# A two-block model on one core: order of ScalarE's table loads in the HGRN recurrence, three weight casts moved, nine filler matmuls and a bank turn

## What is computed

```python
# block 1
u = rms_norm(h, norm_mix_w)
q_a, k_a, v_a, f_a, q_h, f_h, i_h, g_h, gate_a, gate_h = split(u @ w_in)
y_a = forgetting_attention(...) @ w_attn_out                   # 8 heads of 64
f_val = lb + (1 - lb) * sigmoid(f_h); log_f = log(f_val); k = 1 - f_val
o_h = hgrn2_recurrence(q_h, log_f, k, i_h)                     # 8 heads of 128
o_h = rms_norm(o_h, hgrn_norm_w) * sigmoid(g_h)
mixed = sigmoid(gate_a) * y_a + sigmoid(gate_h) * (o_h @ w_hgrn_out)
h = h + mixed @ w_o
h = h + hierarchical_moe(rms_norm(h))                          # 32 experts, top 2
x = rms_norm(h)[:, 16:]
# block 2
h = h + 0.5 * rmsnorm(swiglu(rmsnorm(h, n0), ffn1_wi, ffn1_wo), n1)     # 2816 wide
h = h + rmsnorm(hybrid_mixer(rmsnorm(h, n2)), n3)   # Fourier, short conv, delta net
h = h + 0.5 * rmsnorm(swiglu(rmsnorm(h, n4), ffn2_wi, ffn2_wo), n5)
```

## Time and profile before

| | |
|---|---|
| Runs | 2757.00, 2758.17, 2758.91 us |
| Median | 2758.17 us |
| Profiled execution, its own time | 2753.36 us |
| Its span in the trace | 2752.0 us |
| Mean granted PE clock | 0.989 of full |
| PE busy | 2632.0 us, 96% |
| PEld busy | 2069.1 us, 75% |
| DVE busy | 1288.1 us, 47% |
| ACT busy | 888.8 us, 32% |
| ACT_TABLE_LOAD | 78 times 1283 ns |

### The profile page before, as it was taken

The page is one execution under the profiler, slowest core; times in us unless marked ns, Lnnn a source line. Parts: engine busy times, 40 slices in busy tenths (PEclk is TensorE's granted clock), DMA queues, the critical chain, the costliest instruction groups (busy, mean ns, idle before and its releaser), DMA issues.

```text
span 2752.0 us, 38590 instructions
## 1 busy us (share of the span) xinstructions
PE 2632.0 (96%) x16264; PEld 2069.1 (75%) x16264; DVE 1288.1 (47%) x2277; ACT 888.8 (32%) x1320; POOL 148.9 (5%) x201
## 2 busy tenths in 40 slices
PE   8999999999999989999999999999999999899997
PEld 6778787778744333359999999888979776688885
DVE  4446566534423333355343465454444433644444
ACT  4334445333221111133222242444435322431322
POOL 0000000000100000000000000132140400000000
PEclk9999999999999999999999999999999999999998
DMA  4012111134599999963222222211111122223221
GB/s 142 16 63 67 57 58 62 58 138 137 208 412 420 421 420 420 420 279 110 86 93 93 78 83 76 96 51 58 51 58 51 61 90 93 92 92 98 93 88 58
DMA packets 78203, 381.62 MB, mean 139 GB/s; under 512 B 9944, under 2 KB 10200, under 8 KB 52816
## 3 DMA queue, kind: packets, MB, share of 16 engines
q1 hardware_dynamic: 71856, 357.14, 35.3%
q0 software_dynamic: 5456, 20.11, 1.9%
q10 hardware_dynamic: 720, 1.90, 0.2%
HBM read 372.67 MB, written 10.62 MB: 139 GB/s over the span
## 4 chain that ended last, share of the span: by engine, by line
PE 74%; DMA 8%; DVE 4%; ACT 2%; SPq 2%; issue 1%; DVEq 0%; POOLq 0%; ACTq 0%
PE ps L208 72%; DMA rmore<-in_w_ein 5%; DMA ring<-in_w_ein 2%; SPq L293 2%; PE ps L212 1%; ACT L218 1%; DVE ringr L581 0%; DMA vrow<-uT 0%; PE ps L1958 0%; DMA ring<-in_w_hg 0%; DVE uT L472 0%; DVE hT L2660 0%; ACT ringr L575 0%; DMA xg<-vrow,idx 0%; ACT hdd L1227 0%
## 5 line engine op out<-in xcount | busy, mean ns | idle before, releaser
L208 PE MATMUL ps<-uh,ringr 128*128 128x264 f32 (+1 forms) x2256 | 552.7, 340 | 7.2 <-DVE mgb L3946 5.1
L208 PEld LDWEIGHTS ps<-uh,ringr 128*128 128x128 f32 x2256 | 366.2, 189 | 50.9 <-issue 8.6
L208 PE MATMUL ps<-buh,ringr 128*128 128x512 f32 (+1 forms) x1312 | 347.0, 351 | 10.0 <-ACT hg L1209 8.9
L208 PE MATMUL ps<-uTr,ringr 128*128 128x512 f32 (+1 forms) x1136 | 351.3, 346 | 0.0
L581 DVE TENSOR_TENSOR ringr<-ring,ringr 128x1024 fp32r<-128x1024 f32 (+1 forms) x215 | 258.2, 1212 | 141.8 <-ACT ringr L575 141.5
L208 PEld LDWEIGHTS ps<-buh,ringr 128*128 128x128 f32 x1312 | 218.7, 189 | 41.1 <-issue 13.0
L575 ACT CAST ringr<-ring 128x1024 fp32r<-128x1024 f32 (+1 forms) x215 | 219.3, 1036 | 87.2 <-DMA ring<-in_w_fi 33.5
L208 PEld LDWEIGHTS ps<-uTr,ringr 128*128 128x128 f32 x1136 | 197.7, 189 | 22.8 <-issue 3.1
L208 PE MATMUL ps<-ful,ringr 128*128 128x264 f32 (+1 forms) x648 | 169.6, 322 | 0.2 <-DVE ful L508 0.2
L2621 DVE TENSOR_TENSOR fsg<-ps,fsg 128x528 f32<-128x528 f32 (+1 forms) x44 | 30.8, 700 | 198.5 <-PE ps L208 195.1
L208 PE MATMUL ps<-fhh,ringr 128*128 128x264 f32 (+1 forms) x576 | 123.6, 321 | 0.0
(11 more groups left out here) (485 smaller groups left out, 4557.9 us busy)
## 6 DMA issues: line engine op xcount, KB each, us to landing
rmore<-in_w_ein SPq DMA_DIRECT2D x51, 1024.0 KB, 27.0
eahead<-in_w_ein SPq DMA_DIRECT2D x47, 1024.0 KB, 26.7
ring<-in_w_ein SPq DMA_DIRECT2D x30, 1024.0 KB, 27.0
rmore<-in_w_eout SPq DMA_DIRECT2D x27, 1024.0 KB, 27.0
ring<-in_w_fi SPq DMA_DIRECT2D x54, 512.0 KB, 3.7
ring<-in_w_eout SPq DMA_DIRECT2D x19, 1024.0 KB, 27.3
eahead<-in_w_eout SPq DMA_DIRECT2D x18, 1024.0 KB, 27.1
fmore<-in_w_fi SPq DMA_DIRECT2D x34, 512.0 KB, 3.8
```

The lines of the kernel that those rows point to most:

```text
L208: return self.P.matmul(out, lhsT, rhs, start=start, stop=stop, skip_group_check=True)
```

## The change

The tanh table is loaded right behind the logarithm in `project_act`. The root leaves `output_act` (beat 7) and becomes a method of its own, called at beat 6 between the two groups of steps. `Ffn.act` casts pieces 4, 5 and 6 before the norm's root. Nine filler matmuls stand before the first product of round 1 in `ConvFourier.pe`. In `MixerEnd.pe` the turn is set to 2 ahead of the eight products, so that the first takes banks 4 and 5.

```diff
@@ Hgrn.act
                 if h >= 2:
                     self.output_act(h - 2, n)
                 fill(STEPS[h][0])
+                if h >= 2 and n == 6:
+                    self.root_act(h - 2)
                 if h < 9 and n == 7:
                     self.turn_act(h - 1)
                 fill(STEPS[h][1])
@@ Hgrn.project_act
         A.activation(self.lf, self.fs, ACT.Ln).then_inc(self.f_log.next(), 1)
+        k.table(ACT.Tanh)
         for _ in range(5):
             yield 1
@@ Hgrn.output_act
-        if n == 7:
-            k.table(ACT.Ln)
-            A.wait_ge(*self.sum.at(h + 1))
-            if h:
-                A.wait_ge(*self.fin.at(h))
-            rb = k.rb[:, 0:S]
-            A.activation(rb, k.ps[:, self.bank["sum", h], :], ACT.Ln, bias=k.eps[:, 0:1], scale=1.0 / 128).then_inc(
-                self.o_log.next(), 1)
-            A.wait_ge(*self.o_log.last())
-            A.activation(rb, rb, ACT.Exp, scale=-0.5).then_inc(self.root.next(), 1)
+
+    def root_act(self, h):
+        k, A = self.k, self.k.A
+        k.table(ACT.Ln)
+        A.wait_ge(*self.sum.at(h + 1))
+        if h:
+            A.wait_ge(*self.fin.at(h))
+        rb = k.rb[:, 0:S]
+        A.activation(rb, k.ps[:, self.bank["sum", h], :], ACT.Ln, bias=k.eps[:, 0:1], scale=1.0 / 128).then_inc(
+            self.o_log.next(), 1)
+        A.wait_ge(*self.o_log.last())
+        A.activation(rb, rb, ACT.Exp, scale=-0.5).then_inc(self.root.next(), 1)
@@ Ffn.act
-        W.ahead_act(0, 5)
+        for i in range(4, 7):
+            W.cast_act(i)
         self.norm.root_act()
@@ ConvFourier.pe
         for j in range(4):
+            if j == 1:
+                k.busy(7, 9)
             for x in (3, 0, 1, 2) if j else (2,):
@@ MixerEnd.pe
         k.busy(banks[0], 9)
+        k.turn = 2
         for m in range(8):
```

## The result

The changed kernel took **2725.1 us** (median of four runs, 2724.83 to 2726.81) against 2757.6 us for the kernel before (four runs, 2755.94 to 2758.91): ratio 0.9884, 95% interval 0.9867 to 0.9901. The forecast was 2731.1 us, its range 2726 to 2741. The direction was right; the medians are 32.5 us apart where 27.1 were forecast.

What follows compares the result with a forecast made beforehand. PE, busy 96% of the span, was taken as the bound, gaining only where it waits or runs at lower clock. Terms summed to 27.1 us: 2753.36 to 2726.3 profiled, 2758.17 to 2731.1 us median; range 2726 to 2741.

Steps and rivals of the forecast that it cites:

- 1. to 3., recurrence: Odd passes: tanh load earlier 5.1 us, root earlier 3.1 us, full clock in pass 3 1.6 us; 9.8 us.
- late weight cast: Recurrence, odd passes: a late weight cast or DVE ends the wait for hg next, leaving 2.6 of 5.1 us.
- Terms 1 and 2: Recurrence: tanh load ahead in passes 1, 3, 5, 7 gains 5.1 us; root ahead in passes 3, 5, 7 gains 3.1.
- 4. New loads at nothing: Recurrence: eight loads behind hlf cost nothing, given 2.56 us idle in pass 4 and 3.4 us cover in pass 3.
- 5. First feed-forward: First feed-forward: three casts before the root remove PE's 2.00 us wait; gain 2.0 us, bounds 0.8 and 2.0.
- 6. Second: Second feed-forward: the casts remove the 7.76 us wait and the half clock behind it; 10.6 us, bounds 6 and 10.6.
- 7. Convolution: Convolution: nine fillers keep the clock up behind a wait of 2.69 us that stays; 2.9 us, bounds 0 and 2.9.
- 8. Bank turn: Mixer's end: first w_o2 product no longer waits for the last gated tile; 1.8 us, bounds 0.5 and 4.2.
- The Trainium skill's price of a load: Rival, odd passes: a load costs 2.66 us, nearly all 8.9 us of waits go; 30.7 us gained, 2727.5 us; 2%.

Runs made afterwards that it cites:

- More loads in the new place: The changed kernel with two more table loads (silu, sigmoid) ahead of the new one behind each of the eight hlf: 2735.7 us, ratio 0.9932.

## Why the prediction missed, step by step

**The step that failed is the last one of the sum**, the way from the profiled execution to the median: "It lay 4.8 us under the median of the three runs; the same difference from the median gives 2731.1 us". It took three runs for the centre of the kernel before, and their distance from one profiled execution for a constant that the changed kernel would have too. In 46 later runs the centre is 2753.4 us, which is where the profiled execution lay, and only eight are as slow as 2755.9 us or more, as all four first ones were. The changed kernel's eight runs lie within 2722.8 to 2726.8 us, and its profile on their median. Without the 4.8 us the forecast is 2726.3 us, 1.2 above the measured median. The range had the same flaw: 1.9 us for how runs differ came from the same three, where the spread is 11 us. Why the first four all fell high stays open: with eight in 46 that slow, four in a row would be a chance of about one in a thousand (an estimate), so the draws as the later runs show them hardly explain it, and no run shows another cause. The changed kernel took the same time in its first four runs as in the later ones (2725.1 and 2725.3 us).

**Terms, forecast and measured** (profiles; against the second profile of before in brackets). That the sum came out 1.1 us from the profiled difference is in part luck: the bank turn brought 2.1 us more than its term and the recurrence 0.7 less, and 1.3 us went the other way between T8 and M, by a draw of the clock that no term speaks of.

1. to 3., recurrence: 9.8, and 8.8 + 0.3 = 9.1 [9.9]. Passes 3, 5 and 7 came as forecast. Pass 1 gave 0.3 us and not its 1.28: behind the next weight cast, which waits for its DMA, PE waits for `hQl` (rows below), the "late weight cast" of the lower bound. Terms 1 and 2 are not separate as the sum had them: the load's part alone shows no gain in the time, and in its one profile half-clock stretches behind the root's remaining waits took back half of what the passes gained.
4. New loads at nothing: right by what the waits show, and closer than I thought. The 3.4 us of cover in pass 3 said little; the even passes have 1.24 us left.
5. First feed-forward: 2.0, and 2.3 [3.8].
6. Second: 10.6, and 10.7 [9.8].
7. Convolution: 2.9, and 2.8 [0]. Right in this draw, worth half on the mean.
8. Bank turn: 1.8, and 3.9 [5.0]. The mis-sized term: I expected the clock to fall in the pieces, and left out the nine fillers that stand directly ahead of them. It stayed at 1.00 there, and the stage came near the upper bound of 4.2. The experiment without the fillers shows the fall, in one profile.

ACT and PE in pass 1 of the changed kernel (timeline):

```profile
244.43 1.05 ACT L575 CAST ringr<-ring 128x1024 fp32r<-128x1024 f32 x1 [2.12 <-DMA ring<-in_w_hg]
...
249.01 1.08 PE L208 MATMUL ps<-hQl,hKl 128*128 128x64 f32 x8 [0.47 <-DVE hQl L1348]
```

The expert stage ran on as before, 481.97 us against 482.04, only earlier. The -1.28 us from T8 to M are the wait of 2.99 us that was there before, with a longer half-clock stretch behind it in this draw.

**The Trainium skill's price of a load**, 2.66 us with a drain of about 1.38 us ("ScalarE: Activation LUTs", section "What ACT_TABLE_LOAD costs"), is not what the rows of "More loads in the new place" show: three loads in a row and the ACTIVATE behind them start 1.28 to 1.30 us apart. The measurement decides.

## To carry to other kernels

Before forecasting a median from a profile, count the half-clock stretches of the profile and ask which of them are bound to come: here a stretch behind a wait of 1 to 3 us came in one execution and not in the next, some 1 to 3 us each, and a handful of them is worth more than several terms of a sum. Others came each time (in pass 3, and behind the recurrence), and those are safer to count. Where a profiled execution and the median of three runs lie 4.8 us apart, don't carry the distance over as a constant: the three runs may not show the centre. A short wait that PE pays for another engine's read right behind its own product adds up: eight of 0.82 to 0.87 us were 6.7 us here, and work of PE that could be issued in between gave 6.9 us.

## What the runs showed of the hardware

The granted clock does not follow from the program alone. The same stretch with the same wait of 2.69 us ran at 0.67 in one execution and at 1.00 in another, and a stretch at 50 to 60 us fell in three of the fourteen profiles with the same code ahead of it. Not every wait is such a draw: behind the wait of 2.99 us that follows the recurrence the clock fell in eleven profiles of eleven. Twelve fillers (2.84 us) inside that wait kept it at 1.00 in three of three. Nine (2.17 us) inside the convolution's wait kept it in nine of nine, where it fell in three of five without. Nine directly ahead of the broken-up work at the mixer's end kept it in eight of nine.

A table load took 1.28 us, also three in a row, with 1.28 to 1.30 us from start to start. In the even passes one more of them was covered (PE's wait went from 0.31 to 0.36 us at most), a second was not (1.65 us).
